# Experts of a mixture-of-experts layer: scatter and gather spread over the steps, rows added straight into x, one overflow branch behind the result

## What is computed

```python
def moe_swiglu(h, router, w1, w3, w2):
    ...
    logits = (h @ router).astype(jnp.float32)
    top_v, top_i = lax.top_k(logits, TOP_K)
    gates = jax.nn.softmax(top_v, axis=-1).astype(h.dtype)
    ...
    xb = h_ext[row_tok].reshape(n_blocks, MOE_BLOCK, D)

    def expert_block(args):
        xe, e = args
        return swiglu(xe, w1[e], w3[e], w2[e])

    yb = lax.map(expert_block, (xb, block_e))
    y = jnp.zeros((T + 1, D), h.dtype).at[row_tok].add(yb.reshape(n_rows, D) * row_w[:, None])
    return y[:T]
...
x = x + g2_l * f[:B * L].reshape(B, L, D)
return rms_norm_2(x, final_g)
```

## Time and profile before

| | before |
|---|---|
| median of 3 runs | 2320.93 us (2320.70 to 2323.35) |
| the profiled execution's own time | 2321.37 us |
| its span in the trace | 2320.0 us |
| TensorE busy (matmul) | 2161.9 us, 93% |
| TensorE weight loads | 1911.6 us, 82% |
| VectorE busy | 1687.3 us, 73% |
| ScalarE busy | 1263.9 us, 54% |
| GpSimd busy | 41.3 us, 2% |
| mean granted TensorE clock | 0.953 of full |
| read from HBM | 577.56 MB, 249 GB/s |

### The profile page before, as it was taken

One profiled execution on the slowest core, in us unless ns is written; L12 is line 12 of the kernel. 1 busy time (PEld: TensorE's weight loads), 2 busy tenths in 40 slices (PEclk: granted clock), 3 DMA queues, 4 the chain that ended last, 5 costly groups with the idle time before them and its releaser, 6 DMA issues.

```text
span 2320.0 us, 31037 instructions
## 1 busy us (share of the span) xinstructions
PE 2161.9 (93%) x12897; PEld 1911.6 (82%) x12897; DVE 1687.3 (73%) x1785; ACT 1263.9 (54%) x1267; POOL 41.3 (2%) x78
## 2 busy tenths in 40 slices
PE   8999999899899979999998899999999899999994
PEld 8887899899887758999987687877788787878784
DVE  1477687789766564877546688886888688888884
ACT  2347653455333334443344576766777676767673
POOL 3001000000000000000000000000000000000000
PEclk8899999899899988999997999999999999999997
DMA  8473476567753332988725799997999899999991
GB/s 285 159 223 112 142 245 204 160 211 239 252 179 109 109 109 88 309 286 264 239 83 199 264 352 340 371 330 286 360 350 364 290 344 340 371 328 369 331 371 50
DMA packets 332809, 580.82 MB, mean 250 GB/s; under 512 B 10357, under 2 KB 150155, under 8 KB 332656
## 3 DMA queue, kind: packets, MB, share of 16 engines
q1 hardware_dynamic: 329152, 572.57, 71.0%
q0 software_dynamic: 3008, 5.78, 1.1%
q10 hardware_dynamic: 496, 0.33, 0.1%
HBM read 577.56 MB, written 1.07 MB: 249 GB/s over the span
## 4 chain that ended last, share of the span: by engine, by line
PE 80%; DVE 10%; ACT 5%; issue 4%; DMA 0%; DVEq 0%; SPq 0%; ACTq 0%
PE bk L635 13%; PE bk L637 13%; PE bk L636 13%; PE bk L629 9%; PE bk L630 8%; PE bk L631 8%; DVE wlo L1791 3%; ACT whi L1225 2%; DVE macc L1818 2%; PE bk L714 2%; PE bk L700 1%; PE bk L1129 1%; DVE uc L2133 1%; PE bk L943 1%; PE bk L1094 1%
## 5 line engine op out<-in xcount | busy, mean ns | idle before, releaser
L1791 DVE TENSOR_TENSOR wlo<-raw,whi 128x2048 fp32r<-128x2048 f32 x475 | 1080.5, 2277 | 310.6 <-ACT whi L1225 309.9
L1225 ACT CAST whi<-raw 128x2048 fp32r<-128x2048 f32 x475 | 901.4, 1899 | 442.2 <-PE bk L637 296.7
L629 PE MATMUL bk<-HH,whi 128*128 128x256 f32 x1544 | 456.2, 295 | 11.3 <-DVE HL L1864 8.3
L630 PE MATMUL bk<-HL,whi 128*128 128x256 f32 x1544 | 446.0, 289 | 0.0
L631 PE MATMUL bk<-HH,wlo 128*128 128x256 f32 x1544 | 445.6, 289 | 0.0
L635 PE MATMUL bk<-whi,xh 128*128 128x512 f32 x896 | 359.8, 402 | 22.4 <-DVE MO L2436 18.3
L637 PE MATMUL bk<-wlo,xh 128*128 128x512 f32 x896 | 355.2, 396 | 0.0
L636 PE MATMUL bk<-whi,xl 128*128 128x512 f32 x896 | 352.9, 394 | 0.0
L629 PEld LDWEIGHTS bk<-HH,whi 128*128 128x128 f32 x1544 | 306.2, 198 | 19.1 <-issue 16.4
L630 PEld LDWEIGHTS bk<-HL,whi 128*128 128x128 f32 x1544 | 306.3, 198 | 1.7 <-issue 1.0
L631 PEld LDWEIGHTS bk<-HH,wlo 128*128 128x128 f32 x1544 | 305.7, 198 | 0.0
(11 more groups left out here) (369 smaller groups left out, 2596.8 us busy)
## 6 DMA issues: line engine op xcount, KB each, us to landing
raw<-in_moe_w SPq DMA_DIRECT2D x336, 1024.0 KB, 5.5
raw<-in_ada_w SPq DMA_DIRECT2D x48, 1024.0 KB, 5.3
raw<-in_ff_w SPq DMA_DIRECT2D x40, 1024.0 KB, 5.5
raw<-in_w_in SPq DMA_DIRECT2D x29, 1024.0 KB, 5.4
raw<-in_w_mod SPq DMA_DIRECT2D x24, 1024.0 KB, 5.3
raw<-in_w_up SPq DMA_DIRECT2D x22, 1024.0 KB, 5.2
raw<-in_attn_w_qkv SPq DMA_DIRECT2D x12, 1024.0 KB, 5.6
raw<-in_w_branch SPq DMA_DIRECT2D x8, 1024.0 KB, 5.4
```

What stands on the lines that cost most here:

```text
L629: pe.matmul(o, sh, mh, start=start, stop=False, skip_group_check=True)
L630: pe.matmul(o, sh, ml, start=False, stop=False, skip_group_check=True)
L1225: act.copy(whi[k][:, :n], raw[q.slot[i]][:, :n]).then_inc(q.hi_done.mark(g), 1)
L1791: dve.tensor_tensor(wlo[k][:, :n], raw[q.slot[i]][:, :n], whi[k][:, :n].bitcast(F), ALU.subtract).then_inc(q.taken.mark(i), 1)
```

## The change

1. **Scatter spread.** The scatter of an expert no longer stands in one piece. Its four pieces of two chunks go to the steps n = 1 to 4 of the next expert, one in each, and VectorE's additions with them.
2. **Gather spread.** The 8 chunks go to the steps i = 4 to 7 of the pair before, two in each; the transposes and gate sums go to i = 12; `pb` is made at i = 2, right behind `dve_count` in the first pair.
3. **Banks.** `up` has a ring of its own, (0, 1, 2); scatter, gather, `turn`, `count`, `ptt` and `gs` share the ring (3, 4, 5). The last scatter has six banks.
4. **First turn.** The `turn` of step 0 moves from the end of step 0 into step 1, behind the first `up` of it.
5. **Rows straight into x.** `MO` and its memset are gone. Each scatter bank is added by VectorE as X = bank x gate + X, in two instructions of 256 columns where there was one of 512. The first pieces of a scatter need only the first half of `YL`.
6. **Result ahead.** The result is written out before any branch. ScalarE's table for Ln and Exp is loaded before the last `act_collect`. Behind the result stands one single `If`; the three overflow blocks and a second writing of the result are its body. The engines wait ahead of it only for the count, not for each other.

```diff
-        M_G, M_T = (0, 1, 2, 3), (4, 5)
+        M_G, M_T = (0, 1, 2), (3, 4, 5)
...
             for s_, (e, n) in enumerate(steps):
-                yield from pe_up(st, s_, e // 2, e % 2)
+                p, i = divmod(s_, 14)
+                yield from pe_up(st, s_, p, e % 2, 0)
+                if s_ == 1:
+                    yield from pe_turn(st, 0)
+                yield from pe_up(st, s_, p, e % 2, 1)
                 if s_:
                     yield from pe_down(st, s_ - 1)
-                if n == 1 and e:
-                    yield from pe_scatter(st, e - 1, (e - 1) // 2, (e - 1) % 2)
+
+                if e and 1 <= n <= 4:
+                    yield from pe_scatter(st, e - 1, (e - 1) // 2, (e - 1) % 2, 2 * n - 2, M_T)
...
-                if n == 3 and e % 2 == 0 and e + 2 < NEXP:
-                    yield from pe_gather(st, e // 2 + 1, M_G, M_T, lambda n, tb, p=e // 2 + 1: ro(tb, 7)[:, 2 * p + n:2 * p + n + 1])
-                yield from pe_turn(st, s_)
+                if p < 3 and 4 <= i < 8:
+                    yield from pe_gather(st, p + 1, M_T, (2 * i - 8, 2 * i - 7))
+                if p < 3 and i == 12:
+                    yield from pe_gather_rest(st, p + 1, M_T, lambda n, tb, p=p + 1: ro(tb, 7)[:, 2 * p + n:2 * p + n + 1])
+                if s_:
+                    yield from pe_turn(st, s_)
             yield from pe_down(st, len(steps) - 1)
-            yield from pe_scatter(st, 7, 3, 1)
+            for c in range(0, 8, 2):
+                yield from pe_scatter(st, 7, 3, 1, c, (0, 1, 2, 3, 4, 5))
...
+            act.preload_act_table_set("natural_log_exp_and_others")
...
-                dve.tensor_tensor(MO[:, c:c + 2, :], chunks2(u.t), MO[:, c:c + 2, :], ALU.add).then_inc(u.sem, 1)
+            for m in range(2):
+                t = dve.scalar_tensor_tensor(out=X[:, c + m, :], in0=u.t[:, m * S:(m + 1) * S], scalar=modT[3][:, 40 + c + m:41 + c + m],
+                                             in1=X[:, c + m, :], op0=ALU.mult, op1=ALU.add)
...
-                if n == 1 and e:
-                    yield from dve_scatter(st, e - 1)
-                if n == 2 and e == 0:
+                if 1 <= n <= 4 and e:
+                    yield from dve_scatter(st, e - 1, 2 * n - 2)
+                if s_ == 2:
                     yield from dve_count()
-                if n == 3 and e % 2 == 0 and e + 2 < NEXP:
-                    yield from dve_gather_pair(st, e // 2 + 1, lambda n, tb, p=e // 2 + 1: RK[:, tb, 2 * p + n:2 * p + n + 1])
-                yield from dve_turned(st, s_)
+                if p < 3 and i == 2:
+                    yield from dve_pb(st, p + 1, lambda n, tb, p=p + 1: RK[:, tb, 2 * p + n:2 * p + n + 1])
+                if p < 3 and i == 12:
+                    yield from dve_gs(st, p + 1)
...
-        for j in range(3):
-            with nc.If(n_over > j):
...
+        with nc.If(n_over > 0):
+            for eng in (pe, act, dve, pool, sp):
+                for told in ends:
+                    eng.wait_ge(*told)
+            for j in range(3):
+                over(j)
+            again()
+        sp.wait_ge(*all_out)
```

More of the change, by code:

```diff
@@ L1089, in pe_gather @@
             pe.wait_ge(*(yield from dve_step.of("pb", q.name, p)))
-            for c in range(8):
-                u = take(ring_g, "gx", q.name, p, c)
+            for c in chunks:
+                u = take(ring, "gx", q.name, p, c)
                 for n, src in enumerate((TH, TL)):
@@ L1095, in pe_gather, with pe_gather_rest @@
                 t.then_inc(u.fill(), 1)
-            u = take(ring_t, "ptt", q.name, p)
+        def pe_gather_rest(q, p, ring, gate):
+            u = take(ring, "ptt", q.name, p)
             for n in range(2):
@@ L1191, in pe_over @@
             yield from pe_down(q, 7 * j + 6)
-            yield from pe_scatter(q, j, j, 0)
+            for c in range(0, 8, 2):
+                yield from pe_scatter(q, j, j, 0, c, M_T)
         def pe_main():
@@ L1680, in act_route, with act_gather @@
             act.activation(col(3), col(2), AF.Exp).then_inc(act_step.mark("gap"), 1)
-        def act_gather(q, p, both):
-            for c in range(8):
+        def act_gather(q, p, chunks, both):
+            for c in chunks:
                 act.wait_ge(*(yield from B.full("gx", q.name, p, c)))
@@ L2488, in dve_experts @@
                     g += 1
+                    if s_ == 1 and k == 1:
+                        yield from dve_turned(st, 0)
                     if k == 3:
@@ L2503, in dve_experts @@
             yield from dve_collect(st, 7, 3, 1)
-            yield from dve_scatter(st, 7)
+            for c in range(0, 8, 2):
+                yield from dve_scatter(st, 7, c)
         def dve_over(q, j):
@@ L2521, in dve_over @@
             yield from dve_collect(q, j, j, 0)
-            yield from dve_scatter(q, j)
+            for c in range(0, 8, 2):
+                yield from dve_scatter(q, j, c)
         def dve_main():
@@ L2562, in sp_result, with engine @@
                                  onat[:, tb, half * 512:half * 512 + 512]).then_inc(arrived, 16)
-            sp.wait_ge(arrived, n)
-        run(sp_main(), pool_main(), pe_main(), act_main(), dve_main())
-        ends = [st.slab_done.now(), xhi_done.now(), xlo_done.now(), dve_step.now(), pool_step.now(), B.fills[3].now(), N.at["gain",]]
+        final = {c: ("x_moe", "w", 7, c) for c in range(0, 8, 2)}
+        def engine(*parts):
+            for part in parts:
+                yield from part
@@ L2603, in build @@
[L2603 to L2608 removed]
+        B = Banks(banks, [sem(f"over_filled{i}") for i in range(8)], [sem(f"over_drained{i}") for i in range(8)])
+        xhi_done, xlo_done, dve_step = (Count(sem(f"over_{n}")) for n in ("x_hi_done", "x_lo_done", "dve_step"))
+        q.steps = [(0, n) for j in range(3) for n in range(7)]
@@ new lines, in again @@
+        def again():
+            nonlocal B, dve_step, act_step
+            B = Banks(banks, [sem(f"last_filled{i}") for i in range(8)], [sem(f"last_drained{i}") for i in range(8)])
+            dve_step, act_step = Count(sem("last_dve_step")), Count(sem("last_act_step"))
+            run(sp_result(), pe_result({}), act_result(), dve_result())
+            sp.wait_ge(*dma_sems["out"])
+        with nc.If(n_over > 0):
+            for eng in (pe, act, dve, pool, sp):
+                for told in ends:
+                    eng.wait_ge(*told)
+            for j in range(3):
+                over(j)
+            again()
```

182 lines of the change are left out of this document (88 added, 94 removed).

## The result

The changed kernel takes 2255.31 us (median of four runs, 2251.45 to 2259.52) against 2321.19 us of the kernel before on the same chip: ratio 0.9715 [0.9691, 0.9739], 65.9 us less. The prediction was 2260 us, 2251 to 2272. The four runs lie at two levels, 2251.5 and 2259. With the ten runs of the same kernel further down (`again`, `again_b`) the median of fourteen is 2257.5 us, so some 2 of the 65.9 us are luck.

The account below looks back on a forecast made before the run. TensorE was taken to bound plain steps of 17.05 us, leaving gains only around them. Terms 24.8 + 22.5 + 8.1 - 0.8 - 11.0 + 17.0 = 60.6 us off 2321.4, less 0.4 for the median, gave 2260 us, range 2251 to 2272.

Parts of the forecast that it names:

- Scatters: Steps behind the seven inner scatters: `up` no longer waits for VectorE's addition, nor does the clock fall; 24.8 us won.
- gathers and count: Three gathers: waits and half clock go, 22.5 us won; behind the count, four `pb` instructions delay `wlo`, 0.8 us lost.
- first turn: Turn of step 0: two slabs ahead of it cover the wait for VectorE's product; 8.1 us won.
- ring (3, 4, 5): n = 4 of experts 2 and 4: four banks needed, turn waits 3.9 us plus 1.6 for clock; 11.0 us lost.
- plain steps: Expert steps without side work: the prediction had no term for them, so no gain.
- end: Behind the last expert: earlier adds, fewer table loads, result ahead of one slow branch; 17.0 us won.
- rival 4: All 28 scatter-piece steps: turn or `up` waits for VectorE and clock falls, 125 us lost, 2385 us; chance 0.02.
- Rival 1: Scatter-piece steps: VectorE's 0.9 us isn't hidden and delays `wlo`, TensorE loses 12 us; around 2269 to 2275, chance 0.14.
- Rival 2: Ring steps and end: no clock loss and a quick branch, 2255.5 us; 2249 with VectorE ahead; chance 0.13.
- Rival 3: Expert part's slab supply: DMA can hold only 336 GB/s, so only the end is won, 2304 us; chance 0.03.

Follow-up runs that it names:

- again: The changed kernel once more with no edit, as control: 2257.03 us, ratio 0.9728 to the kernel before; in a second group 2258.98 us, 0.9730.
- whole: The changed kernel with each scatter and gather in one piece again, in the old rings; end and first turn stay changed: 2293.74 us.
- oldrings: The changed kernel with pieces still spread, but in the old rings, pieces sharing four banks with `up`: 2251.71 us.
- ringfix: The changed kernel with gather chunks at i = 5, 6, 7, 12 and transposes at i = 13, so no step takes four ring banks: 2244.55 us.
- dvex: The changed kernel with two more unused 512-column VectorE additions behind each of the 28 scatter pieces: 2266.87 us.
- best_b: The changed kernel with ringfix's edit and the count's VectorE work cut in four parts, steps 2 to 5; repeat measurement: 2236.35 us, ratio 0.9640.
- late: The changed kernel with gather chunks at i = 8 to 11, beside scatter pieces, so twelve steps take four ring banks: 2314.47 us.
- turn0: The changed kernel with the turn of step 0 back at the end of step 0: 2265.11 us, ratio 0.9761.

## Why the prediction was right

The mechanisms were as forecast, but for one reason under *Scatters*, and so were the sizes. By steps from turn to turn in both traces, with plain steps of 17.03 us before and 16.98 after (means of eleven):

| term | forecast | measured | how |
|---|---|---|---|
| scatters | +24.8 | +24.6 | before 7 x 1.93 of work, 4 x 2.88 and 3 x 4.53 behind them; after 28 x 0.50 |
| gathers and count | +22.5 - 0.8 | +22.5 | before 44.3 over plain in three steps; after 12 x 0.94, 3 x 1.25 and 6.8 |
| first turn | +8.1 | +8.0 | interval 19.58, now 11.55 |
| ring (3, 4, 5) | -11.0 | -11.8 | 2 x 3.85, and 2.4 + 1.7 in the steps behind |
| plain steps | 0 | +2.9 | 55 x 0.053 |
| end | +17.0 | +18.0 | windows |
| **sum** | **60.6** | **64.2** | 64.4 by the windows |

So the expert part and the end gave 3.6 us more than forecast, most of it from plain steps, which had no term. Taken from 2321.2 the 64.2 give 2257.0 us, near the 2257.5 of the fourteen runs; that the first four had a median 1.7 lower is luck, in all likelihood the front's. The first turn's term was read from a row of the chain, which has the turn of step 1 at 1274.36; its first matmul starts at 1274.19, so the interval is 19.58 us and not 19.75.

*Scatters.* No `up` waits for a piece, and the clock stays full. `whole` shows that the loss comes back when the places are undone; it undoes the rings as well, but `oldrings` shows that the old rings alone bring none of it back. The reason that I gave, `up` in a ring of its own, was more than is needed: `oldrings` has no such ring and no such wait. Of the two reasons in my text, the one that rival 4 was argued against with, banks filled a step earlier, is the one that holds.

*Gathers.* Work 5.0 us each, forecast 5.2. TensorE no longer waits for `pb`, and it works at full clock.

*Count.* The wait for `wlo` went from 4.1 to 4.9 us, as the four instructions of `pb` said.

*Ring.* The wait is in the steps named, for the addition named, of the length forecast (3.9; 3.85 measured). The 1.6 for the clock was 2.4 and 1.7 in this execution, and in `again` one of the two was missing. Without the ring's steps the kernel has `ringfix`'s time: the term was a real loss, which the change had brought with itself.

*End.* 16.5 us from the last `down` matmul, forecast 17.5. The last scatter's 16 matmuls went at full clock (2235.24 to 2237.4 in the timeline, 3.53 us before at half clock; the forecast had kept that pace), and the transposes began at 2238.50, 4.9 us behind the `down`, not 6. The Trainium skill ("Runtime: NRT & Kernel Launch", Instruction fetch mechanics) has a far branch wait for a fetch. In the trace's records SyncE's register load starts at 2246.53, its branch at 2247.55, and its next instruction at 2250.07: 2.5 us, of the slow kind that I took (2.94), and 2.5 to 2.8 in the ten other profiles of changed kernels. An 8 KB packet of an instruction queue starts in it, at 2248.48. So the trace agrees with the page. The result's last bytes had landed by 2249.41 in the records, 0.7 us before the end. The view of DMA has them in slices of 0.15 us of the last 6.1, then the stores after, and the stores before (x, KB each, us from issue to landing):

```profile
GB/s 0 0 295 443 295 336 296 309 363 376 403 161 54 40 107 40 228 336 363 376 416 363 416 363 363 175 54 67 40 94 13 13 0 0 0 0 0 0 0 0
...
out<-onat SPq DMA_DIRECT2D x3, 256.0 KB, 3.4
```

```profile
out<-onat SPq DMA_DIRECT2D x4, 256.0 KB, 2.2
```

In all eleven profiles of changed kernels the branch ended the span, 0.5 to 1.2 us behind the last landing. It stands behind SyncE's four store issues, and one of these took 0.6 to 1.8 us (1.20 in the profile after), where each took 0.33 to 0.36 before. So a late issue costs at the end too; why it is late, no run here shows.

*Rivals.* Rival 1 (pieces delay `wlo`) was wrong at 0.87 us a piece and right at 2.15: `dvex`. Rival 2 (the small terms fall well) had the time that came, 2255.5, but not what made it: in this profile the clock fell in both places of the ring and the branch was a slow one. Plain steps (2.9 us), the end (1.0) and the front's luck stand in their place. Rival 3: slabs came at 349 GB/s over the whole expert part, and in `best_b` at 356 with TensorE never idle, so the supply isn't the bound. Rival 4 is `late` in small: twelve such steps in place of 28, at 5.8 us each, where it had 2.85 + 1.6.

What stays open is why a plain step is 0.053 us shorter. It is so in each kernel with the change's code, in `oldrings`, `whole` and `turn0` too (16.96 us), so it is neither the rings nor the places nor the first turn. In the records it lies in `up`: its matmuls start 229.2 ns apart before and 227.5 after (those of `down` 233.3 and 234.0). In the code `MO` is gone in all of them and `onat` and `ssq` stand in its place, so tiles lie elsewhere in on-chip memory; whether that is the cause, no run here shows.

## What to carry to other kernels

Put a piece of side work where the bank that it takes was filled a step or more ago, and then count, step by step, how many banks of the ring are taken by what is filled in that step: one more than the ring has, and the next instruction in line waits for a bank that was filled in the same step (here 3.85 us and up to 2.4 for the clock). Whether the side work has banks of its own matters less than this. The other engines' room in such a step is that of one slab's chain; a long piece on them (here 6 us for the count) lost 6.8 us in one piece and about 1 in four parts.

## What was not expected of the hardware

- The same code takes between 1248.9 and 1259.1 us up to the first turn, in the ten profiles of changed kernels other than `turn0`, and the changed kernel's single times range from 2251.5 to 2260.2. The granted clock of that window is 0.93 or 0.94; 163.8 us of it were at half clock in `best_b` (the longest), 146.8 in the profile after, and half of the difference, 8.5, is most of the 10.0 between the two. Who compares two profiles of one execution each should first subtract what unchanged code gained or lost.
- At waits of 3.7 us on TensorE the clock fell to half, before they ended or within 1.5 us behind, in 12 of 12 cases in `late`, in 8 of 8 in after, again_b, `dvex` and `turn0`, but in 1 of 2 in `again`; at waits of 2.6 us before, in 3 of 7; of 2.8 us in `whole`, in 4 of 7; and of 1.25 us in `oldrings`, in 2 of 3. A length alone didn't decide it.
- The result's stores were 3.4 us from issue to landing (median of three, above), where the same four stores took 2.2 us before.
